# The order of the experts: from the fifth slot on, many and few tokens by turns in place of falling counts

## The chip, the cores and the metric

The kernel runs on one core of one Trainium2 chip. The metric is the device time of one execution in microseconds (us). TensorE is called PE here, VectorE DVE, ScalarE ACT, GpSimd POOL and SyncE SP.

## The reference: one layer of a hybrid decoder, with experts at its end

The layer takes 1024 prompt tokens and 8 tokens of decoding, 1032 rows of 1024 numbers. It norms them, projects them, runs gated linear attention and differential attention, projects back and adds. Then comes the part that the change touches, a mixture of experts: each token chooses one of 4 groups and in it 2 of 4 experts, so that 2064 pairs of token and expert are computed.

```
g = argmax(t @ w_rg + b_rg)
top_v, top_i = top_k(t @ w_re[g] + b_re[g], 2)
gates = softmax(top_v) * p_top
hid = silu(t @ w_gate[e]) * (t @ w_up[e])      # 1024 -> 256, for each chosen expert e
out = sum over e of gates[e] * (hid @ w_down[e])   # 256 -> 1024
x = x + out;  y = rmsnorm(x)
```

Only the tokens of an expert have to be computed for it. The counts of the 16 experts follow from the inputs; they are 140, 69 and 114 for the experts 0 to 2, and of the other thirteen, in falling order, 207, 170, 161, 152, 145, 135, 118, 116, 112, 112, 106, 105 and 102.

## The kernel before

Everything up to the router (about 700 us) is left alone by the change. After it the kernel runs 16 slots, one expert each, written out for every engine with semaphores between them. The experts 0 to 2 have the slots 0 to 2. The other thirteen are ranked on the chip by their number of tokens, and slot 3 takes the one with most, slot 15 the one with fewest. The columns of three tables on the chip go by rank: `tok` (which rows of the tokens to gather), `dest` (where to add the result) and `gtab` (the gate's weight); `sexp` holds the expert's number of each rank.

What is fixed when the kernel is built is the capacity of each slot, `CAPS` (line 38): 208 for the slots 0 to 2, then 212, 200, 188, 176, 164, 152, 140 and from slot 10 on 128. A capacity over 128 means two parts (`parts`, line 116), the second holding the rest: two gathers, two scatters, two parts of the down product. Tokens beyond a capacity would go to an overflow pass, which isn't taken with these inputs as the ranks' counts are all within it.

A slot e does the following, each engine in this order:

- SP (L747) loads the weights in f32, 3 MB per expert in three transfers, into two staging buffers: gate and up for slot e+3 once those of slot e+1 are split, down for slot e+2 once that of slot e is split.
- POOL issues the gather for slot e+3 (L918, from `h_scratch` in HBM, rows of 4 KB), then the scatter of slot e (L930, which adds rows of 4 KB into `sum_scratch` in HBM). A scatter waits for the slot's outputs and for the landing of the scatter before it, since two may add to the same row. So the gather for slot e+3 stands behind the scatter of slot e-1.
- PE computes gate and up for slot e (`split_mm`, L2101 to L2103: three f16 matmuls for one f32 product; 96 matmuls with as many columns as the capacity), transposes the tokens of slot e+1 (L2464, L2467), and computes the down product of slot e-1 (12 matmuls of 512 columns for each part). The second half of the transposes lies within the down product.
- ACT makes silu's exponentials (L1301 to L1305), the high half of the hidden product (L1309), reads half of the transposed tokens (L1291), splits weights for slot e+2 (L1233) and down for slot e+1 (L1238) into f16, and writes half of the output (L1323).
- DVE makes the hidden product (L1977, L1979), its low half (L1982), reads the other half of the tokens (L1965), writes half of the output (L1992) and makes the low halves of the split weights (L1803, L1808; three of 2.3 us per slot).

Two of PE's waits depend on the capacity. A slot of 128 needs one PSUM bank for gate and up (`one_bank`, line 131), and two such slots in a row use different banks, so that the second may start before the hidden product of the first is made (`hidden_before`, line 557). Otherwise gate and up of slot e wait for the hidden product of slot e-1.

After slot 15's scatter has landed, `sum_scratch` is loaded again, normed and written out.

Of the kernel before, what the change touches and what calls it, by code (L numbers as in the profile page):

```python
# [15 lines left out]
ALU = mybir.AluOpType  # L16
# [3 lines left out]
P = 128  # L20
D = 1024
# [12 lines left out]
NG, EPG, NE = 4, 4, 16  # L34
FF = 256
FIXED = 3
CAP_TOP, CAP_STEP = 212, 12
CAPS = [208] * FIXED + [max(P, CAP_TOP - CAP_STEP * j) for j in range(NE - FIXED)]
CAP = max(CAPS)
MORE = 80  # L40
FULL = FIXED + 1
# [108 lines left out]
def build(nc, I, O):  # L150
    ctx = ExitStack()
    with ctx:
# [131 lines left out]
        tok = sb("tok", [P, COLS + NOV], I32)  # L284
# [351 lines left out]
        def _(sp):  # L636
# [103 lines left out]
            def expert(e):  # L740
                if e < FIXED:
                    return slice(e, e + 1)
                return bass.ds(sp.value_load(sexp[0:1, e:e + 1], min_val=0, max_val=NE - 1), 1)

            def load(w, sub, x, s, sems):
                src = I[w][0, x].rearrange("e (k p) f -> p (e k) f", p=P)
# [72 lines left out]
        def _(pool):  # L819
# [93 lines left out]
            def gather(e):  # L913
                if e >= 2:
                    pool.wait_ge(s_eT, 4 * (e - 1))
                for g, r in parts(e):
                    rows_at = bass.IndirectOffsetOnAxis(ap=tok[0:r, 2 * e + g:2 * e + g + 1], axis=0)
                    pool.indirect_dma_start(out=xg[0:r, e % 2, g, :], out_offset=None, in_=h2d[:, :],  # L918
                                            in_offset=rows_at, bounds_check=T, oob_is_err=False
                                            ).then_inc(s_gx[e % 2], 16)  # L920

            def scatter(e):
                pool.wait_ge(s_ya, e + 1)
                pool.wait_ge(s_yv, e + 1)
                if e:
                    pool.wait_ge(s_yo[(e - 1) % 2], y_sent(e - 1))
                else:
                    pool.wait_ge(s_x1o, 16 * (NT + 1))
                for g, r in parts(e):
                    pool.indirect_dma_start(out=sumd[:, :], out_offset=bass.IndirectOffsetOnAxis(  # L930
                        ap=dest[0:r, 2 * e + g:2 * e + g + 1], axis=0), in_=yb[0:r, e % 2, D * g:D * g + D],
                        in_offset=None, bounds_check=T - 1, oob_is_err=False, compute_op=ALU.add
                        ).then_inc(s_yo[e % 2], 16)

# [36 lines left out]
        def _(act):  # L971
# [322 lines left out]
            def slot(e):  # L1294

                s = e % 2
                if e != NE:
                    c = CAPS[e]
                    g = eg[:, 0:2 * c]
                    act.wait_ge(s_gup, e + 1)  # L1300
                    act.activation(g, gate_up(e)[0], ACT.Exp, scale=-ISC2).then_inc(s_sg, 1)  # L1301
                    act.wait_ge(s_sg, 3 * e + 1)
                    act.activation(g, g, ACT.Ln, bias=1.0).then_inc(s_sg, 1)
                    act.wait_ge(s_sg, 3 * e + 2)
                    act.activation(g, g, ACT.Exp, scale=-1.0).then_inc(s_sg, 1)  # L1305
                    if e != NE - 1:
                        read_tokens(e + 1, 0)
                    act.wait_ge(s_hf, e + 1)
                    act.activation(hidh[:, s, :, 0:c], hid[:, 0:2 * c].rearrange("p (f t) -> p f t", f=2),  # L1309
                                   ACT.Copy).then_inc(s_hh2, 1)  # L1310
                    if e != NE - 1:
                        read_tokens(e + 1, 2)
                if e + 2 < NE:
                    split_gate_up(e + 2, 0)
                if e != 0:
                    v = e - 1
                    if e == 1:
                        act.wait_ge(s_route, 1)
                    if e >= 3:
                        act.wait_ge(s_yo[v % 2], y_sent(e - 3))  # L1320
                    for g, r in parts(v):
                        act.wait_ge(s_down, downs(e - 2) + 2 * g + 1)
                        ins = act.activation(yb[0:r, v % 2, D * g:D * g + 512], ps[0:r, 4 + 2 * g, :], ACT.Copy,  # L1323
                                             scale=gtab[0:r, 2 * v + g:2 * v + g + 1])
                    ins.then_inc(s_ya, 1)
                if e + 2 < NE:
                    split_gate_up(e + 2, 1)
                if e + 1 < NE:
                    if e != 0:
                        act.wait_ge(s_down, downs(e - 1))  # L1330
                    split_down(1 - s, 16 * ((e + 1) // 2 + 1))
# [50 lines left out]
        def _(dve):  # L1382
# [585 lines left out]
            def slot(e):  # L1968
# [17 lines left out]
                if e != 0:  # L1986
                    v = e - 1
                    if e >= 3:
                        dve.wait_ge(s_yo[v % 2], y_sent(e - 3))
                    for g, r in parts(v):  # L1990
                        dve.wait_ge(s_down, downs(e - 2) + 2 * g + 2)
                        ins = dve.tensor_scalar(yb[0:r, v % 2, D * g + 512:D * g + D], ps[0:r, 5 + 2 * g, :],  # L1992
                                                gtab[0:r, 2 * v + g:2 * v + g + 1], None, ALU.mult)
                    ins.then_inc(s_yv, 1)
                if e == 0:
                    dve.wait_ge(s_mlo, 4)
# [586 lines left out]
```

## Time and profile before

| | us |
|---|---|
| median of 3 runs | 966.47 |
| the runs | 966.39 to 970.37 |
| the profiled execution | 968.47 |
| its span, first to last instruction | 966.6 |
| slot 4's gate and up done | 775.91 |
| slot 15's gate and up done | 920.03 |
| last scatter issued | 931.45 |

All times in the text are from the start of the span. In the rows PE's busy time is modelled for pipelined matmuls: the start of one to the start of the next is the better measure. A timeline row has the start, the duration, engine and line, the operation with its operands, and in brackets the idle time of the engine before it with what released it.

### The profile page before, as it was taken

The numbers are of one execution on the slowest core, as the hardware profiler recorded it, in microseconds if no ns is written. First come the engines' busy times: TensorE is split into PE (matmuls) and PEld (weight loads), VectorE is DVE, ScalarE is ACT, GpSimd is POOL, SyncE is SP. The second block draws the span as 40 slices with busy tenths as digits, with TensorE's granted clock in tenths as the row PEclk, the third lists the DMA queues.
The fourth block names the chain that finished last, engine by engine and source line by source line (L and its number), as shares of the span: only waits on it lengthen the run. The fifth ranks groups of instructions, "written<-read, shape, count | busy, mean of one in ns | idle before, by whom it ended". The sixth has DMA issues, their size and how long they took to land.

```text
span 966.6 us, 16039 instructions
## 1 busy us (share of the span) xinstructions
PE 829.1 (86%) x6150; PEld 522.9 (54%) x6150; DVE 573.4 (59%) x932; ACT 424.8 (44%) x767; POOL 262.6 (27%) x173
## 2 busy tenths in 40 slices
PE   4999989779989989977899999995289999997920
PEld 3766634346556644324566755552277878765710
DVE  6632687747774531158788734335675767776815
ACT  5520230245651311235567614433436666775714
POOL 2104993640521000002000000000424465443312
PEclk9999999979998999996899999998579999998975
DMA  8326766301031268863000024423866889999647
GB/s 298 90 65 198 238 222 201 126 0 45 1 93 50 83 223 247 254 236 110 1 1 2 1 76 164 135 108 114 287 210 208 270 265 298 314 295 335 187 96 307
DMA packets 99073, 155.86 MB, mean 161 GB/s; under 512 B 13704, under 2 KB 63384, under 8 KB 98994
## 3 DMA queue, kind: packets, MB, share of 16 engines
q1 hardware_dynamic: 91170, 132.92, 41.6%
q0 software_dynamic: 6208, 18.17, 7.7%
q10 hardware_dynamic: 1616, 3.70, 1.0%
q8 instruction: 50, 0.82, 0.4%
q14 instruction: 29, 0.24, 0.1%
HBM read 129.25 MB, written 28.86 MB: 164 GB/s over the span
## 4 chain that ended last, share of the span: by engine, by line
PE 47%; DVE 12%; DMA 12%; issue 10%; SPq 7%; ACT 6%; POOL 6%; POOLq 0%; ACTq 0%; DVEq 0%
PE ps L2101 12%; PE ps L2102 11%; PE ps L2103 11%; DMA sum_scratch<-kv,dest 5%; POOL kv L860 4%; SPq L727 3%; SPq L728 2%; PE ps L2383 2%; DMA hT_reg<-h_scratch,tok 2%; DVE w_reg L1418 2%; DMA w_reg<-in_w_up 2%; DVE mxs L1725 2%; DMA gt<-q_scratch 1%; DVE dg_reg L2093 1%; PE ps L2371 1%
## 5 line engine op out<-in xcount | busy, mean ns | idle before, releaser
L930 POOL DMA_INDIRECT sum_scratch<-kv,dest x26 | 72.2, 2777 | 117.4 <-DMA sum_scratch<-kv,dest 74.5
L2101 PE MATMUL ps<-hT_reg,w_reg 128*128 128x344 f16 (+1 forms) x312 | 98.1, 314 | 4.6 <-DVE hT_reg L1430 2.7
L2102 PE MATMUL ps<-hT_reg,w_reg 128*128 128x344 f16 (+1 forms) x312 | 98.0, 314 | 0.0
L2103 PE MATMUL ps<-hT_reg,w_reg 128*128 128x344 f16 (+1 forms) x312 | 97.8, 313 | 0.0
L860 POOL TENSOR_TENSOR kv<-kv,gt 128x1024 f32<-128x1024 f32 x32 | 82.9, 2621 | 53.4 <-DMA kv<-in_cache_k 53.4
L2101 PE MATMUL ps<-w_reg,hT_reg 128*128 128x512 f16 (+1 forms) x216 | 83.5, 386 | 8.6 <-ACT kv L1099 4.9
L2102 PE MATMUL ps<-w_reg,hT_reg 128*128 128x512 f16 (+1 forms) x216 | 83.4, 386 | 0.0
L2103 PE MATMUL ps<-w_reg,hT_reg 128*128 128x512 f16 (+1 forms) x216 | 83.0, 384 | 0.0
L888 POOL TENSOR_TENSOR rst<-rst,neghalf 128x1 f32<-128x1 f32 (+3 forms) x27 | 18.8, 698 | 233.3 <-DVE rst L1706 233.3
L1195 ACT ACTIVATE hT_reg<-ps,mxn 128x128 f32<-128x128 f32 (+7 forms) x64 | 47.1, 739 | 50.0 <-DVE mxn L1726 46.3
L2101 PE MATMUL ps<-hT_reg,dg_reg 128*128 128x128 f16 (+4 forms) x256 | 55.1, 239 | 1.4 <-DVE hT_reg L1965 1.4
L1471 DVE TENSOR_REDUCE gbc<-kv 128x16 f32<-128x1024 f32 x32 | 38.6, 1215 | 29.5 <-POOL kv L860 29.5
L2101 PE MATMUL ps<-hT_reg,mix_reg 128*128 128x128 f16 (+5 forms) x256 | 54.3, 238 | 2.1 <-DVE hT_reg L1965 2.1
L2102 PE MATMUL ps<-hT_reg,dg_reg 128*128 128x128 f16 (+4 forms) x256 | 55.1, 239 | 0.0
L2103 PE MATMUL ps<-w_reg,mix_reg 128*128 128x512 f16 (+1 forms) x144 | 54.6, 379 | 0.0
L2101 PE MATMUL ps<-w_reg,mix_reg 128*128 128x512 f16 (+1 forms) x144 | 54.6, 379 | 0.0
L2102 PE MATMUL ps<-w_reg,mix_reg 128*128 128x512 f16 (+1 forms) x144 | 54.6, 379 | 0.0
L2103 PE MATMUL ps<-hT_reg,mix_reg 128*128 128x128 f16 (+5 forms) x256 | 54.2, 238 | 0.0
L2102 PE MATMUL ps<-hT_reg,mix_reg 128*128 128x128 f16 (+5 forms) x256 | 54.2, 238 | 0.0
L1725 DVE TENSOR_REDUCE mxs<-ps 128x1 f32<-128x640 f32 (+7 forms) x48 | 45.7, 951 | 10.2 <-PE ps L2349 7.0
L1445 DVE TENSOR_SCALAR dg_reg<-ps 128x512 f32<-128x512 f32 (+2 forms) x16 | 9.9, 619 | 64.6 <-PE ps L2103 64.6
L2383 PE MATMUL ps<-dg_reg,hT_reg 128*128 128x128 f32 x288 | 41.4, 293 | 4.3 <-DVE mix_reg L620 2.7
(379 smaller groups left out, 2117.1 us busy)
## 6 DMA issues: line engine op xcount, KB each, us to landing
kv<-in_cache_k SPq DMA_DIRECT2D x64, 256.0 KB, 3.2
w_reg<-in_w_gate SPq DMA_DIRECT2D x16, 1024.0 KB, 5.7
w_reg<-in_w_up SPq DMA_DIRECT2D x16, 1024.0 KB, 13.3
w_reg<-in_w_down SPq DMA_DIRECT2D x16, 1024.0 KB, 14.0
w_reg<-in_w_in SPq DMA_DIRECT2D x12, 1024.0 KB, 7.4
mix_reg<-in_cache_v SPq DMA_DIRECT2D x32, 256.0 KB, 3.2
kv<-in_cache_v SPq DMA_DIRECT2D x32, 256.0 KB, 3.2
mix_reg<-in_x_prompt SPq DMA_DIRECT2D x8, 512.0 KB, 8.5
```

The source lines that it names most:

```text
L727: page = sp.value_load(ptab[0:1, i:i + 1], min_val=0, max_val=n_pool - 1)
L728: sp.dma_start(vq[VBUF[k]][:, j], cv[bass.ds(page, 1)].rearrange("n p c -> p (n c)")).then_inc(s_vp[VBUF[k]], 16)
L860: pool.tensor_tensor(pg, pg, qbc[:, b % 2].unsqueeze(1).to_broadcast([P, 2, 512]), ALU.mult).then_inc(s_kq, 1)
L930: pool.indirect_dma_start(out=sumd[:, :], out_offset=bass.IndirectOffsetOnAxis(ap=dest[0:r, 2 * e + g:2 * e + g + 1], axis=0), in_=yb[0:r, ...
L1195: act.activation(prob[:, u % 3, m, 0:n], scores(u, m), ACT.Exp, scale=DK ** -0.5 * ISC2, bias=mxn[:, u % 2, m:m + 1], accum_out=rsum[:, i ...
L1418: dve.scalar_tensor_tensor(w_slot(slot_l, n), w_stage(n), SC, w_slot(slot_h, n), ALU.mult, ALU.subtract).then_inc(s_wl, 1)
L1471: dve.tensor_reduce(dsc[:, b, 2 * s:2 * s + 2], kv4[:, s].rearrange("p (g m d) -> p g m d", g=2, m=8), AX, ALU.add).then_inc(s_kh, 1)
L1725: link(dve.tensor_reduce(mxs[:, u % 2, ms], sc, AX, ALU.max))
L2101: pe.matmul(out, lh, rh, start=start, stop=False)
L2102: pe.matmul(out, lh, rl, start=False, stop=False)
L2103: return pe.matmul(out, ll, rh, start=False, stop=stop)
L2383: ins = pe.matmul(ps[:, 6 + i % 2, DV * h:DV * h + DV], wT[:, v % 2, j], vd[:, j, DV * h:DV * h + DV], start=j == 0, stop=j == i)
```

## The change

The ranks and their capacities stay, now as `RANKED`. A new list `PLACE` says which rank each slot takes: 0, 1, 2, 3, 4, 10, 5, 11, 6, 12, 7, 13, 8, 14, 9, 15. `CAPS` of the slots follows from it: 208, 208, 208, 212, 200, 128, 188, 128, 176, 128, 164, 128, 152, 128, 140, 128. Where a table is read, its column is now that of the slot's rank. The gathers, the scatters, the loads and the matmuls are otherwise the same ones.

```
-CAPS = [208] * FIXED + [max(P, CAP_TOP - CAP_STEP * j) for j in range(NE - FIXED)]
+RANKED = [208] * FIXED + [max(P, CAP_TOP - CAP_STEP * j) for j in range(NE - FIXED)]
+PLACE = [0, 1, 2, 3] + [r for pair in zip(range(4, 10), range(10, NE)) for r in pair]
+CAPS = [RANKED[r] for r in PLACE]
...
-                return bass.ds(sp.value_load(sexp[0:1, e:e + 1], min_val=0, max_val=NE - 1), 1)
+                return bass.ds(sp.value_load(sexp[0:1, PLACE[e]:PLACE[e] + 1], min_val=0, max_val=NE - 1), 1)
...
-                    rows_at = bass.IndirectOffsetOnAxis(ap=tok[0:r, 2 * e + g:2 * e + g + 1], axis=0)
+                    rows_at = bass.IndirectOffsetOnAxis(ap=tok[0:r, 2 * PLACE[e] + g:2 * PLACE[e] + g + 1], axis=0)
...
-                        ap=dest[0:r, 2 * e + g:2 * e + g + 1], axis=0), in_=yb[0:r, e % 2, D * g:D * g + D],
+                        ap=dest[0:r, 2 * PLACE[e] + g:2 * PLACE[e] + g + 1], axis=0), in_=yb[0:r, e % 2, D * g:D * g + D],
...
-                                             scale=gtab[0:r, 2 * v + g:2 * v + g + 1])
+                                             scale=gtab[0:r, 2 * PLACE[v] + g:2 * PLACE[v] + g + 1])
...
-                                                gtab[0:r, 2 * v + g:2 * v + g + 1], None, ALU.mult)
+                                                gtab[0:r, 2 * PLACE[v] + g:2 * PLACE[v] + g + 1], None, ALU.mult)
```

## Rows read from the trace of the kernel before

**Rows 1.** The page's slices, 40 equal ones: the DMA engines' busy tenths.
```profile
DMA  8326766301031268863000024423866889999647
```
**Rows 2.** Windows: stretch, its us, busy of each engine, clock, DMA share, GB/s.
```profile
775.91:790.99 15.08, 14.64 (x157) 11.82 (x154) 10.84 (x10) 10.02 (x11) 9.53 (x5) 1.00 0.87 277
...
859.96:872.10 12.14, 11.89 (x136) 8.32 (x136) 9.84 (x11) 9.13 (x11) 6.01 (x3) 1.00 0.96 283
...
883.08:898.95 15.87, 11.93 (x128) 8.95 (x129) 9.78 (x11) 8.80 (x11) 7.10 (x4) 0.78 1.04 345
...
909.31:920.03 10.72, 9.34 (x125) 7.19 (x123) 7.27 (x9) 4.98 (x9) 1.56 (x1) 1.00 0.46 68
...
776.00:909.00 133.00, 122.69 (x1401) 92.96 (x1398) 98.16 (x96) 92.95 (x107) 63.46 (x33) 0.97 0.97 302
```
**Rows 3.** Timeline of PE, slots 10 to 12.
```profile
863.84 0.38 PE L2101 MATMUL ps<-mix_reg,gt 128*12 128x512 f16 x1
...
866.53 0.23 PE L2101 MATMUL ps<-hT_reg,mix_reg 128*128 128x128 f16 x1
...
871.85 0.22 PE L2103 MATMUL ps<-hT_reg,mix_reg 128*128 128x128 f16 x1
874.03 0.62 PE L2464 MATMUL ps<-ident,hT_reg 128*128 128x128 f16 x8 [1.96 <-DMA hT_reg<-h_scratch,tok]
...
877.52 0.22 PE L2101 MATMUL ps<-hT_reg,dg_reg 128*128 128x128 f16 x1
```
**Rows 4.** Timeline of PE behind slot 12's gate and up.
```profile
887.02 1.03 PE L2464 MATMUL ps<-ident,hT_reg 128*128 128x128 f16 x8 [3.98 <-DMA hT_reg<-h_scratch,tok]
...
892.95 0.38 PE L2102 MATMUL ps<-mix_reg,gt 128*128 128x512 f16 x1
```
**Rows 5.** What PE waited for, 775 to 930: us in total, times, longest.
```profile
PE ps L2464 <- DMA hT_reg<-h_scratch,tok: 8.4, 5, 4.0
```
**Rows 6.** Timeline of POOL: scatters (L930) and one gather (L918).
```profile
785.56 6.52 POOL L930 DMA_INDIRECT sum_scratch<-kv,dest  x1 [4.63 <-DMA sum_scratch<-kv,dest]
...
802.86 4.22 POOL L930 DMA_INDIRECT sum_scratch<-kv,dest  x1 [6.29 <-DMA sum_scratch<-kv,dest]
807.38 1.51 POOL L930 DMA_INDIRECT sum_scratch<-kv,dest  x1 [0.30 <-issue]
...
873.20 2.25 POOL L930 DMA_INDIRECT sum_scratch<-kv,dest  x1 [6.62 <-DMA sum_scratch<-kv,dest]
875.75 1.37 POOL L930 DMA_INDIRECT sum_scratch<-kv,dest  x1 [0.30 <-issue]
877.43 1.09 POOL L918 DMA_INDIRECT hT_reg<-h_scratch,tok  x1 [0.31 <-issue]
884.35 2.66 POOL L930 DMA_INDIRECT sum_scratch<-kv,dest  x1 [5.84 <-DMA sum_scratch<-kv,dest]
...
895.27 2.80 POOL L930 DMA_INDIRECT sum_scratch<-kv,dest  x1 [6.89 <-DMA sum_scratch<-kv,dest]
...
915.69 1.56 POOL L930 DMA_INDIRECT sum_scratch<-kv,dest  x1 [7.03 <-DVE kv L1992]
924.67 1.56 POOL L930 DMA_INDIRECT sum_scratch<-kv,dest  x1 [7.42 <-DVE kv L1992]
931.45 1.56 POOL L930 DMA_INDIRECT sum_scratch<-kv,dest  x1 [5.21 <-DMA sum_scratch<-kv,dest]
```
**Rows 7.** Timelines of DVE and, between its two rows, of ACT.
```profile
788.30 2.28 DVE L1808 SCALAR_TENSOR_TENSOR mix_reg<-w_reg,mix_reg 128x2048 f16<-128x2048 f32 x1
...
833.48 0.42 ACT L1301 ACTIVATE junk<-ps 128x304 f32<-128x304 f32 x1 [3.42 <-PE ps L2103]
...
835.42 0.47 DVE L1979 SCALAR_TENSOR_TENSOR junk<-ps,junk 128x304 f32<-128x304 f32 x1
```
**Rows 8.** DMA queues, 776 to 883: MB and share of 16 engines.
```profile
q1 hardware_dynamic: 17870, 23.47, 64.8%
q0 software_dynamic: 3030, 8.77, 32.5%
```

## The prediction

> **What bounds the kernel now.** I read the page's slices first. Up to 700 us nothing that the change touches runs; from 776 us to about 900 us the DMA engines are full [rows 1]. Then I cut the stage of the experts at the ends of the gate and up products, one stretch for each slot (a stretch ends where ScalarE's first activation of that slot, L1301, starts). Slot 4's products are done at 775.91, slot 15's at 920.03. Look at the busy time of PE beside the sum: 14.64 of 15.08 us in slot 5, but 11.93 of 15.87 in slot 13, and beside it the DMA share, 0.97 from 776 to 909 [rows 2]. So PE sets the pace of the slots with two parts, and something with the DMAs that of the short ones at the end.
>
> What PE waits for there is named by the waits: the gather of the tokens, 8.4 us in five waits, 4.0 the longest [rows 5]. POOL's timeline tells why a gather is late [rows 6]. POOL issues, in order, the gather for slot e+3, then the scatter of slot e, and each scatter waits until the one before it has landed. The scatter of slot 9 was issued at 873.20 and 875.75, the gather behind it at 877.43, and PE could transpose at 887.02, after 3.98 us of idleness [rows 4, 6]. That is a third bound beside PE and the DMA engines: the chain of scatters, on whose back the gathers ride.
>
> **The work of the change, by engine.** The same 16 experts are computed with the same 16 capacities, so the counts of instructions stay: 26 gathers, 26 scatters, 48 loads, 96 matmuls per slot for gate and up. The look-up of the expert's number reads another column; the cost is nothing. Slots 0 to 4 keep their capacities. From slot 5 on the order 188, 176, 164, 152, 140, then six of 128, becomes 128, 188, 128, 176, 128, 164, 128, 152, 128, 140, 128.
>
> *PE alone.* Gate and up take 96 matmuls: 5.36 us at 128 columns (866.53 to the last at 871.85), so 0.042 us per column, 7.9 at 188 [rows 3]. Each part of the down product takes 2.6 to 2.7 us (863.84 to 866.53) [rows 3]. A short slot's transposes and down product take 3.49 us (874.03 to 877.52) [rows 3]. The stretch of slot e holds its own transposes (0.9 us, 1.5 with a second part), the down product of slot e-2 and its own gate and up; with 0.6 us of small waits this gives 15.0 for slot 5 of before (15.08 seen) and 12.0 for slot 11 (12.14 seen) [rows 2]. A short slot behind a short one needs 9.45. In the new order slot 5 needs 12.0, slots 6, 8, 10, 12 and 14 need 15.0, 14.5, 14.0, 13.55 and 13.05, and slots 7, 9, 11, 13 and 15 need 9.45 each: 129.4 us, to be set against 144.1 seen (132.0 by the same prices, the 2.6 between them being a down part that moves behind slot 15). The idle time on offer is therefore about 12 us, half of it in slot 13 alone.
>
> *The tail.* Slot 14 now has two parts. Behind slot 15's gate and up the next scatter came 4.64 us later (920.03 to 924.67) and the last 6.78 after it [rows 2, 6]. Add a down part (2.6) and a second scatter's issue (1.5 and a gap of 0.3): 15.8 instead of 11.4, 4.4 us more. The reload and final norm behind the last scatter stay as they are.
>
> *The DMA engines.* From 776 to 883 queue 1 moved 23.47 MB in 64.8% of 107 us, 2.95 us per MB; queue 0 moved 8.77 MB in 32.5%, 3.97 us per MB [rows 8]. A slot's weights (3.15 MB) need 9.3 us. Counting the tokens of each expert from the inputs, slots 3 to 15 of before have 207, 170, 161, 152, 145, 135, 118, 116, 112, 112, 106, 105 and 102; a row of 4 KB is gathered and scattered, so 112 rows need 3.6 us and 161 rows 5.2. A short slot asks for 12.9 us, a long one for 14.5. A pair asks for 27.4 where PE asks for 24.5. With 0.97 of 133 us used, the new order can fill 4 us at most.
>
> *The chain of scatters.* Slot 4's starts at 802.86, slot 9's at 873.20: five steps of two parts, 14.07 each. Slot 10's at 884.35, slot 11's at 895.27: a step of one part is 10.92 [rows 6]. A pair takes 25.0, more than PE's 24.5 to 22.5. Slots 0 to 4 are unchanged, so slot 4's scatter stays at 802.86; slot 14's then comes after five steps of either kind, 927.8. The weights are in by then, and the quiet steps were near 9 us (915.69 to 924.67), so I take 1.9 off: 925.9. The last follows after 6.78 + 1.8, at 934.5, against 931.45: 3.0 us later.
>
> *The gathers behind it.* The gather for slot 8 follows slot 4's scatter: both parts are issued by about 810.6, as long behind it as now (4.5 + 0.3 + 1.5, then the gathers), and land some 8 to 10 us later (877.43 to 887.02 is 9.6 [rows 4, 6]), say at 819. PE, faster by then, ends slot 7 at 775.91 + 12.0 + 15.0 + 9.45 = 812.4. It waits 6 us. The last such gather, slot 14's: slot 10's scatter at 802.86 + 3 x 14.07 + 3 x 10.92 = 877.8, gathers to 885.5, landed 895.1, then transposes 1.5, down 5.2 and gate and up 5.8: slot 14 done at 907.6, slot 15 at 917.1, and with the tail of 15.8 the end of the scatters is at 932.9.
>
> *The clock.* After PE had idled 3.98 us the granted clock of that stretch was 0.78, of levels 1.2 and 2.4 GHz, and the down product and transposes ran at half speed from 887.02 to about 893: 2.9 us lost [rows 2, 4]. After the 1.96 us at 874.03 it stayed whole [rows 3]. Waits of 6 us will cost that at least once in the last pairs: 932.9 becomes 935.8, 4.4 us later than now.
>
> *Bank sharing.* Two short slots in a row now use a bank each, and gate and up of a slot may start before the hidden product of the one before. No two are adjacent any more, so PE waits for it each time. Behind the products of a long slot PE has 3.5 us of transposes and one down part [rows 3], and the hidden product is there 2.4 us after the end of gate and up (slot 8, 833.48 to 835.42 + 0.47) [rows 7]. The 1.1 us between them hide it, so I cost it at nothing; were VectorE late by all of the 2.4, it would be 1.3 us for each of five slots, 6.5 in all, and it can't be a gain, since the matmuls may never start sooner for it.
>
> **Two rules of the Trainium skill.** Scatters of long slots take POOL several us: slot 3's from 785.56 for 6.52, ending 1.5 us after the third of the weight splits on VectorE (788.30 + 2.28) [rows 6, 7]. In the new order the scatters of the long slots again fall into these splits, so I keep 14.07 for the step; were POOL free of it as in the quiet tail (4.22 us against 1.56 [rows 6]), 2.7 us would go off each of five steps, the chain would end some 13 us earlier, and the DMA engines would be the limit. The Trainium skill ("SBUF — State Buffer", section "A bandwidth-pool intuition that's wrong (but worth ruling out)") says that GpSimd can't write its descriptors while VectorE holds the shared port. By that rule, too, the wait stays, and the trace agrees in kind; its wait behind VectorE's end is 0.1 us there, 1.5 here. The second rule is named with the first rival.
>
> **The rivals.** *The regimes mix and PE sets the pace.* For it: PE's 12 us of idleness lie nearly all in slots 10 to 15, where short slots stand together. Slot 15 would be done at 905.3 and the last scatter start at 921.1, 10.3 us sooner: 956.2. Against it: a DMA share of 0.97 and the order of POOL. Chance 0.17. The Trainium skill ("Perfetto Trace Analysis", section "Optimization Strategy") says that where the most-contended engine changes over time, interleaving the regimes may help; by that rule this rival is the outcome.
>
> *The clock falls in every pair (slower still).* Late gathers for slots 8, 10, 12 and 14 each leave PE idle for over 4 us, and each costs 2.9 us. The chain leaves PE 1.0, 1.5, 2.0 and 2.5 us per pair, so it loses 1.9, 1.4, 0.9 and 0.4, together 4.6 beyond the forecast: 975.1, up to 978 if scatters then start later as well. It decides as soon as the waits pass those 4 us in more than two pairs. Chance 0.25.
>
> *It washes out.* The chain's steps are shorter by 0.3 us each where less is transferred, the full 4 us of DMA time are filled, and the tail takes them back: 966.5, give or take 2. Chance 0.20.
>
> **The numbers.** The profiled execution took 968.47 us (span 966.6), the median of the runs is 966.47; the differences are the same on either. The two ways of counting give +3.0 and +4.4; I take +4.0, 970.5, nearer to the one with the clock in it; chance 0.38, own range 967.5 to 974. What a measurement can tell from no change is about 0.5%, so 961.6 to 971.3 is "same". Faster: the first rival, 0.17. Same: the wash and six tenths of the forecast, 0.43. Slower: the rest of the forecast and the second rival, 0.40. For 8 in 10 the range runs from 959 (into the first rival) to 978 (the second with its late scatters).
>
> **What would show it.** Right: PE idle before the transposes for slots 8, 10 or 12, released by the gather, 4 to 6 us each; scatter starts alternately 14 and 11 us apart from 802.9; DMA share about 1; two or more stretches with a granted clock under 0.85; 15 to 16 us from slot 15's products to the last scatter. Wrong: slot 7 ending at 812 with slot 8's tokens already there, steps of two parts near 11 us, or PE waiting for the hidden product. The steps carry the forecast: if those of two parts shrink to 12, it falls to the first rival.

## The result: slower, by a loop that the prediction did not close

| | before | changed |
|---|---|---|
| median of the runs, us | 966.43 | 980.04 |
| the runs, us | 965.17 to 970.37 | 974.36 to 983.11 |
| the profiled execution, us | 968.47 | 983.11 |
| its span, us | 966.6 | 981.3 |
| slot 4's products done | 775.91 | 776.29 |
| slot 15's products done | 920.03 | 932.68 |
| last scatter issued | 931.45 | 946.72 |

The ratio of changed to before is 1.0106, with a 95% interval from 1.0061 to 1.0151; the quotient of the two medians would be 1.0141, and the four runs of the changed kernel spread over 9 us. A repetition (below) gave 1.0193, from 1.0150 to 1.0236. So the changed kernel is slower by 1 to 2%. 970.5 was predicted, in a range that ended at 978: by the first ratio the result is 976.7, just inside it; by the median of 980.0 and by the repetition it lies past its end.

Between two executions of this kernel the work ahead of the experts may end some us apart, so the measure for a mechanism here is the *stage*: from the end of slot 4's products to the last scatter. It took 155.5 us before and 170.4 after, 14.9 more; the two spans differ by 14.7, so in the profiled executions all of the loss lies in it.

**The stage, slot by slot.** Windows of the changed kernel, cut where ScalarE's first activation of a slot starts. The columns are those of [rows 2]; the lines are slots 7, 9, 10, 11, 12 and 14, then the stretch of the last window of [rows 2], drawn out to 924.

```profile
803.20:816.62 13.42, 10.69 (x124) 8.16 (x124) 7.64 (x9) 9.20 (x10) 6.20 (x5) 0.87 1.06 330
...
831.31:841.25 9.94, 9.12 (x124) 7.08 (x121) 7.46 (x8) 8.90 (x11) 5.12 (x4) 1.00 1.04 285
841.25:862.06 20.81, 16.28 (x156) 12.19 (x157) 12.25 (x12) 9.73 (x12) 8.35 (x3) 0.84 0.84 280
862.06:871.84 9.78, 9.12 (x124) 7.08 (x121) 7.79 (x9) 8.82 (x10) 5.36 (x4) 1.00 1.01 282
871.84:892.53 20.69, 15.60 (x156) 11.45 (x157) 11.74 (x12) 9.65 (x11) 7.53 (x3) 0.84 0.79 272
...
902.16:922.72 20.56, 15.15 (x156) 10.95 (x157) 11.24 (x12) 9.56 (x11) 7.07 (x3) 0.83 0.56 176
...
776.00:924.00 148.00, 127.47 (x1408) 96.67 (x1407) 100.38 (x96) 94.47 (x110) 69.33 (x32) 0.92 0.87 272
```

Slots 9 and 11 took 9.94 and 9.78 us; the price of PE's work alone was 9.45. Slots 10, 12 and 14 took 20.81, 20.69 and 20.56 where that price was 14.0, 13.55 and 13.05, and slot 7 took 13.42 for 9.45. These four are 25.4 us over their prices, out of 27.0 for the eleven slots (156.4 seen, 129.4 priced). Before, the excess was 12.1 over 132.0 [rows 2]. So 2.6 us of work left the slots for the tail, and 14.9 us of idleness and half clock came in. Note the DMA share in the bad stretches, 0.84 and 0.79 (and 0.56 in slot 14, where the weights run out): in the stretches that lose the time, the engines that were to be full are not.

**Who PE waits for.** The waits of PE from 775 to 960 us (total, times, longest), and the four places on its timeline:

```profile
PE ps L2466 <- DMA hT_reg<-h_scratch,tok: 17.9, 4, 5.4
```
```profile
805.90 0.62 PE L2466 MATMUL ps<-ident,hT_reg 128*128 128x128 f16 x8 [2.74 <-DMA hT_reg<-h_scratch,tok]
...
845.78 0.29 PE L2466 MATMUL ps<-ident,hT_reg 128*128 128x128 f16 x1 [4.57 <-DMA hT_reg<-h_scratch,tok]
...
876.93 0.29 PE L2466 MATMUL ps<-ident,hT_reg 128*128 128x128 f16 x1 [5.12 <-DMA hT_reg<-h_scratch,tok]
...
878.29 0.63 PE L2103 MATMUL ps<-mix_reg,gt 128*128 128x512 f16 x1
...
881.92 0.38 PE L2103 MATMUL ps<-mix_reg,gt 128*128 128x512 f16 x1
...
907.57 0.29 PE L2466 MATMUL ps<-ident,hT_reg 128*128 128x128 f16 x1 [5.44 <-DMA hT_reg<-h_scratch,tok]
```

The counterpart of [rows 5]: 17.9 us in four waits, where it was 8.4 in five. The rest of the 25.4, 7.5 us, goes for the most part with the clock: after the wait of 5.12 us a matmul of 512 columns takes 0.63 us at 878.29 and 0.38 at 881.92, and the three long stretches show a granted clock of 0.83 and 0.84, a mean of stretches at the two levels of 1.2 and 2.4 GHz. What a whole clock gives back is measured below.

**Why the gather is late.** POOL's timeline, the counterpart of [rows 6], and DVE's behind it:

```profile
856.74 7.22 POOL L932 DMA_INDIRECT sum_scratch<-kv,dest  x1 [10.21 <-DVE kv L1994]
864.27 1.41 POOL L932 DMA_INDIRECT sum_scratch<-kv,dest  x1 [0.30 <-issue]
865.98 1.08 POOL L920 DMA_INDIRECT hT_reg<-h_scratch,tok  x1 [0.30 <-issue]
867.37 0.97 POOL L920 DMA_INDIRECT hT_reg<-h_scratch,tok  x1 [0.31 <-issue]
874.72 1.63 POOL L932 DMA_INDIRECT sum_scratch<-kv,dest  x1 [6.39 <-DMA sum_scratch<-kv,dest]
...
887.70 7.23 POOL L932 DMA_INDIRECT sum_scratch<-kv,dest  x1 [9.98 <-DVE kv L1994]
...
918.36 7.23 POOL L932 DMA_INDIRECT sum_scratch<-kv,dest  x1 [9.19 <-DVE kv L1994]
...
946.72 1.58 POOL L932 DMA_INDIRECT sum_scratch<-kv,dest  x1 [4.12 <-DMA sum_scratch<-kv,dest]
```
```profile
855.15 0.74 DVE L1994 TENSOR_SCALAR kv<-ps,gtab 48x512 f32<-48x512 f32 x1 [1.88 <-PE ps L2105]
855.82 4.47 DVE L1805 SCALAR_TENSOR_TENSOR mix_reg<-w_reg,mix_reg 128x2048 f16<-128x2048 f32 x2
860.22 2.28 DVE L1810 SCALAR_TENSOR_TENSOR mix_reg<-w_reg,mix_reg 128x2048 f16<-128x2048 f32 x1
...
886.11 0.74 DVE L1994 TENSOR_SCALAR kv<-ps,gtab 36x512 f32<-36x512 f32 x1 [1.87 <-PE ps L2105]
```

Read them as one circle. Slot 8's output is ready when DVE has written it (855.15 + 0.74); its scatter starts at 856.74. By then DVE has gone into three weight splits without a gap, and the scatter takes 7.22 us, until 1.46 us behind the end of the third (862.50). Before, a scatter of a long slot was released by a landing and met the splits midway, with 4.22 us left for it [rows 6]; here it is released by the output itself, each time at the splits' start. The gathers for slot 12 stand behind it, 865.98; PE gets the tokens at 876.93; with transposes and the down product of slot 10 its output is ready, and its scatter starts at 887.70. The circle is 9.24 + 10.95 + 10.77 = 30.96 us, the next one (887.70 to 918.36) 30.66. It leads from slot e to slot e+2, and PE's own work for two slots is 23.45 at that place (14.0 + 9.45). In the new order all long slots of the pairs are of one parity, so every turn of this circle has the two-part scatter, the two-part gather and two down parts in it, and the short slots between have no say.

### The profile page after: what moved, and what is told of

It is laid out like the page before. It is cut to its first block, busy times and chain, and to the rows that moved or that the text cites. A ratio compares the mean times of both kernels' runs of the same rounds, so it can differ in the third digit from the quotient of the medians.

```text
span 981.3 us, 16039 instructions
## 1 busy us (share of the span) xinstructions
PE 834.0 (85%) x6150; PEld 524.6 (53%) x6150; DVE 573.7 (58%) x932; ACT 426.1 (43%) x767; POOL 273.9 (28%) x173
## 4 chain that ended last, share of the span: by engine, by line
PE 45%; DMA 13%; issue 12%; DVE 11%; SPq 7%; POOL 6%; ACT 5%; POOLq 0%; ACTq 0%; DVEq 0%
PE ps L2103 11%; PE ps L2105 11%; PE ps L2104 11%; DMA sum_scratch<-kv,dest 6%; POOL kv L862 4%; DMA hT_reg<-h_scratch,tok 3%; SPq L729 3%; SPq L730 2%; PE ps L2385 2%; DVE w_reg L1420 2%; DMA w_reg<-in_w_up 2%; DVE mxs L1727 2%; DMA gt<-q_scratch 1%; DVE dg_reg L2095 1%; PE ps L2373 1%
## 5 line engine op out<-in xcount | busy, mean ns | idle before, releaser
L932 POOL DMA_INDIRECT sum_scratch<-kv,dest x26 | 82.8, 3186 | 118.9 <-DMA sum_scratch<-kv,dest 62.5
L2103 PE MATMUL ps<-hT_reg,w_reg 128*128 128x344 f16 (+1 forms) x312 | 99.3, 318 | 4.6 <-DVE hT_reg L1432 2.7
L2104 PE MATMUL ps<-hT_reg,w_reg 128*128 128x344 f16 (+1 forms) x312 | 99.2, 318 | 0.0
L2105 PE MATMUL ps<-hT_reg,w_reg 128*128 128x344 f16 (+1 forms) x312 | 99.1, 318 | 0.0
L2103 PE MATMUL ps<-hT_reg,dg_reg 128*128 128x208 f16 (+6 forms) x256 | 59.6, 245 | 0.8 <-DVE hT_reg L1967 0.8
L2104 PE MATMUL ps<-hT_reg,dg_reg 128*128 128x208 f16 (+6 forms) x256 | 59.5, 245 | 0.0
L2466 PE MATMUL ps<-ident,hT_reg 128*128 128x128 f16 x256 | 30.0, 240 | 27.0 <-DMA hT_reg<-h_scratch,tok 20.7
L2103 PE MATMUL ps<-hT_reg,mix_reg 128*128 128x128 f16 (+2 forms) x256 | 49.3, 230 | 2.5 <-DVE hT_reg L1967 2.4
L2104 PE MATMUL ps<-hT_reg,mix_reg 128*128 128x128 f16 (+2 forms) x256 | 49.3, 230 | 0.0
L2105 PE MATMUL ps<-hT_reg,mix_reg 128*128 128x128 f16 (+2 forms) x256 | 49.2, 229 | 0.0
```

The costliest lines, as they stand in the source:

```text
L2103: pe.matmul(out, lh, rh, start=start, stop=False)
L2104: pe.matmul(out, lh, rl, start=False, stop=False)
L2105: return pe.matmul(out, ll, rh, start=False, stop=stop)
L2466: ins = pe.transpose(bank16(kh)[:, c * k:c * k + P], xg[:, s, 0, col:col + P], ident16[:])
```

## The experiments

The theory is **the loop**: a scatter held by the splits on DVE, a gather queued behind it, PE waiting for that gather and then running at half clock. Its rivals: **the DMA engines** (their load in the pairs makes the landings late, wherever the gathers are issued), **the clock alone** (the waits are no worse than before but each costs half speed), **bank sharing** (PE waits for hidden products since no two short slots are adjacent), and **the order itself** (the longer tail and the uneven chain of scatters). The diffs are against the changed kernel, or against the kernel before where the heading says so.

### The changed kernel once more

> The changed kernel again, on the chip and in the rounds of the next three, since its four runs lay 9 us apart. Both theories: 8 to 14 us over the kernel before.

984.17 us beside 966.93; ratio 1.0193 [1.0150, 1.0236]. The waits for gathers are 18.7 us in six, 5.3 the longest; the stage is 171.4 us. POOL again (starts 29.9 and 30.8 us apart):

```profile
861.57 7.22 POOL L932 DMA_INDIRECT sum_scratch<-kv,dest  x1 [10.06 <-DVE kv L1994]
...
891.49 7.23 POOL L932 DMA_INDIRECT sum_scratch<-kv,dest  x1 [9.52 <-DVE kv L1994]
...
922.32 7.23 POOL L932 DMA_INDIRECT sum_scratch<-kv,dest  x1 [9.52 <-DVE kv L1994]
```

So the circle is no accident of one execution.

### Gathers ahead of the scatters, in the changed order and in the one before

```
             gather(2)
+            gather(3)
             for e in range(NE):
-                if e + 3 < NE:
-                    gather(e + 3)
+                if e + 4 < NE:
+                    gather(e + 4)
```

The gather that stood behind scatter e now stands ahead of it: this opens the circle, and no instruction is changed.

> The changed kernel with one gather more ahead of the loop, so that POOL issues the gather for slot e+4, not e+3, before the scatter of slot e. The tokens no longer ride behind a scatter that stands behind the weight splits. Theory A (late gathers, and the clock that falls after each): PE's four waits for a gather (17.9 us) go, the clock stays whole, and with them 7 us in each of the pairs 10/11, 12/13 and 14/15 and 4 us in slot 7; the pace is then the scatters' (25 us a pair) or PE's: 20 to 25 us under the changed kernel at most, 10 at least, so 955 to 970. Rival B (the DMA engines are full, the gathers would land late wherever they are issued): less than 4 us gained. Rival C (the waits for the shared bank): nothing gained.

> The same edit in the kernel before, with its falling order. Theory A: the waits of 8.4 us and the 2.9 us of half clock go, of which some come back as other waits behind the DMA engines: 955 to 960. With the first run it tells what the order alone is worth once the gathers are early: by PE's own pace 0, less the 4.4 us of the tail, so this one is faster than the changed one by 0 to 5 us. Rival B: within 3 us of before.

The changed order: 967.03 us beside 966.93, ratio 0.9982 [0.9955, 1.0008]; the stage shrinks from 171.4 to 150.2 us. The order before: 965.03, ratio 0.9986 [0.9964, 1.0008], stage 151.3. The waits of PE for gathers are gone in both. In the changed order the gain is 12 to 20 us by the ratios (0.9982 against 1.0106 and 1.0193), as the loop had it (10 to 25) and not as the rival of the full DMA engines (under 4). In the order before, the forecast of 955 to 960 was a miss: within 3 us of before is what that rival had given, so this second run alone doesn't speak against it. The changed order's window:

```profile
786.00:925.00 139.00, 130.02 (x1517) 98.45 (x1516) 105.17 (x104) 97.11 (x114) 57.74 (x31) 1.00 0.92 281
```

Clock 1.00 instead of 0.92, DMA share 0.92 instead of 0.87: the DMA engines carry the same traffic in less time when the gathers come early, so their load by itself doesn't set the pace. (How long these gathers took to land, no row shows, since nobody waited for them.) What the two orders differ by without the circle is nothing that this measurement can tell. One thing doesn't add up: the stages are 4 to 5 us shorter than that of the kernel before (155.5), the medians at most 2 us lower. In the profiled executions the difference lies ahead of the stage: the changed order's slot 4 was done at 781.74, that of the kernel before at 775.91, with the same matmuls in front of it. The difference is already there when slot 0 is done (717.31 against 711.54), ahead of all that the change touches; why is open.

### The hold taken away by another instruction

```
-                dve.scalar_tensor_tensor(dst, src, SC, hi, ALU.mult, ALU.subtract).then_inc(s_mlo, 1)
+                dve.tensor_scalar(dst, src, SC, None, ALU.mult).then_inc(s_mlo, 1)
...
-                dve.scalar_tensor_tensor(dst, src, SC, hi, ALU.mult, ALU.subtract).then_inc(s_mld, 1)
+                dve.tensor_scalar(dst, src, SC, None, ALU.mult).then_inc(s_mld, 1)
```

This leaves out the subtraction of the high half.

> The changed kernel with the low half of the split weights made by a tensor_scalar with one input (weight times 64) in place of a scalar_tensor_tensor with two; it leaves out the subtraction of the high half, so the output isn't the reference's. Theory A1 (VectorE's two-input splits keep POOL from writing its descriptors): the first scatter of a long slot takes 1.4 to 1.7 us, not 7.2, the gathers come 5 us sooner, and the kernel is 8 to 15 us faster than the changed one. Rival A2 (POOL waits for something else, or the one-input form holds it as well): these instructions stay at 5 to 7 us and the time within 3 us, unless the new instruction is itself shorter than 2.2 us.

962.20 us, ratio 0.9940 [0.9916, 0.9964], stage 147.1, no wait for a gather. The scatter that took 7.22 us, and the splits:

```profile
852.02 1.21 DVE L1805 TENSOR_SCALAR mix_reg<-w_reg 128x2048 f16<-128x2048 f32 x1
854.26 1.23 DVE L1805 TENSOR_SCALAR mix_reg<-w_reg 128x2048 f16<-128x2048 f32 x1 [1.04 <-issue]
856.16 1.23 DVE L1810 TENSOR_SCALAR mix_reg<-w_reg 128x2048 f16<-128x2048 f32 x1 [0.67 <-ACT mix_reg L1240]
...
853.23 2.35 POOL L932 DMA_INDIRECT sum_scratch<-kv,dest  x1 [7.81 <-ACT kv L1325]
```

As the loop says, and more than the 8 to 15 us that were expected (16 to 24 under the changed kernel by the ratios). But the edit does three things: the instruction reads one operand in place of two, it takes 1.21 us in place of 2.28, and since it is shorter the splits no longer follow without a gap: those at 854.26 and 856.16 start after 1.04 and 0.67 us of idleness. So it doesn't tell a hold by the form of the instruction from one by its length or by the missing gap. The next edit keeps form and length and changes the gap alone.

### The hold taken away by gaps, in both orders

```
                 dve.scalar_tensor_tensor(dst, src, SC, hi, ALU.mult, ALU.subtract).then_inc(s_mlo, 1)
+                if e >= 2:
+                    dve.wait_ge(s_mlo, 2 * e + j + 1)
```

DVE does all of its work, of the same form and length; it only waits for the end of each gate or up split before it issues the next one.

> The changed kernel with a wait on its own semaphore behind each of VectorE's first two weight splits, so that the three no longer run without a gap. Theory A1 (the port passes to POOL only where VectorE leaves a gap): the first scatter of a long slot takes at most 3.8 us (a split of 2.3 and 1.5), not 7.2; the loop scatter, gather, down product, scatter of the long slots falls from 31 us to 27, and the kernel is 8 to 12 us faster than the changed one. If POOL had to wait for the third split for another reason, nothing moves.

> The same two waits in the kernel before. Theory A1: first scatters of at most 3.8 us, the chain of scatters less far behind, its late gathers at slots 12 and 13 a few us earlier: 2 to 6 us faster than before. If the gaps themselves cost (0.1 us, twice a slot, on VectorE's 10 us of 14): within 1 us.

The changed order: 963.58 us beside 968.36, ratio 0.9952 [0.9923, 0.9981], stage 152.8. The order before: 964.34, ratio 0.9945 [0.9910, 0.9979], stage 150.7. Splits and scatter in the changed order:

```profile
788.49 2.28 DVE L1805 SCALAR_TENSOR_TENSOR dg_reg<-w_reg,dg_reg 128x2048 f16<-128x2048 f32 x1
790.80 2.29 DVE L1805 SCALAR_TENSOR_TENSOR gs_reg<-w_reg,dg_reg 128x2048 f16<-128x2048 f32 x1
```
```profile
789.43 2.84 POOL L932 DMA_INDIRECT sum_scratch<-kv,dest  x1 [6.79 <-DVE kv L1996]
...
827.54 2.81 POOL L932 DMA_INDIRECT sum_scratch<-kv,dest  x1 [8.09 <-DVE kv L1996]
```

The first split ends at 790.77, the second starts 0.03 us later, and the scatter is done at 792.27, 1.50 behind the first split; without the gap it was done 1.46 behind the third. No scatter takes over 2.86 us in either order, and no wait for a gather is left. That is the hold, by itself: a gap of 0.03 us lets POOL in. It makes the changed order faster than the kernel before, though nothing of its order, its tail or its traffic is touched. The gain over the changed kernel, 15 to 23 us by the ratios, is more than the 8 to 12 expected, which had counted with a turn of 27 us: the turns of the long slots' scatters were 24.3 and 25.7 us (854.68 to 879.01, and on to 904.70). In the order before the 4 us are within the 2 to 6 expected.

### The clock's share

In slots 9, 11 and 13, behind gate and up, where PE goes idle next:

```
+                    if e in (9, 11, 13):
+                        for _ in range(76):
+                            pe.matmul(ps[:, 0, 0:P], ones16[:], ones16[:], start=True, stop=True)
```

> The changed kernel with 76 spare matmuls of 128 columns (4.2 us, into a bank that nobody reads) ahead of the transposes in slots 9, 11 and 13, where PE waited 4.6 to 5.4 us for a gather; they change no result. Theory A (wait plus clock): the waits shrink to about 1 us, the granted clock of slots 10, 12 and 14 is 1.00 instead of 0.84, and each is 2 us shorter: 5 to 7 us less than the changed kernel. If the clock follows something else, it stays at 0.84 and nothing is gained; if the loop alone sets the pace and the slow clock lies in its shadow, the clock is whole and the gain under 2 us.

980.93 us beside 968.36, ratio 1.0126 [1.0073, 1.0180], stage 168.1. The stretches of slots 10, 12 and 14, here and in the repetition of the changed kernel:

```profile
847.73:867.91 20.18, 18.16 (x232) 14.83 (x230) 12.15 (x12) 9.67 (x11) 8.00 (x3) 1.00 0.82 274
877.70:895.90 18.20, 17.68 (x232) 14.29 (x230) 11.65 (x12) 9.61 (x11) 7.53 (x3) 1.00 0.91 311
...
905.53:924.10 18.57, 17.20 (x232) 13.76 (x230) 11.15 (x12) 9.55 (x12) 7.07 (x3) 1.00 0.60 194
```

They sum to 56.95 us; the repetition had 20.65, 19.65 and 20.71, 61.01. So with a whole clock (1.00) the three stretches are 4.1 us shorter and still 16.4 over their prices of 14.0, 13.55 and 13.05. Of their excess of 20.4 us the clock is a fifth; the circle is the rest. The forecast of 5 to 7 us for the whole was too high: PE still waited 2.0, 0.5 and 1.4 us behind the spare matmuls, the stage is 2.3 to 3.3 us shorter than in the two profiles of the changed kernel, and the ratio (1.0126 against 1.0106 and 1.0193) can't tell a gain from none.

### Bank sharing taken from the kernel before

```
-    return 4 * CAPS[e] <= 512
+    return False
```

> The kernel before with no slot taken as of one bank, so that gate and up of every slot wait for the hidden product of the one before, as they do in the changed kernel. The prediction costs it at nothing: within 0.3% of before. Rival C: up to 6.5 us slower, 1.3 for each of five slots.

970.42 us beside 969.27, ratio 1.0009 [0.9976, 1.0043], stage 157.8. The six short slots in a row lose what the change takes from them, and it costs nothing that can be told (the interval ends at 4 us, and the loss to be explained is 10 to 19). This rival falls.

### Other places for the short slots

```
-PLACE = [0, 1, 2, 3] + [r for pair in zip(range(4, 10), range(10, NE)) for r in pair]
+PLACE = [0, 1, 2, 3, 4, 10, 11, 5, 6, 12, 13, 7, 8, 14, 9, 15]
```

Two short ones and two long ones by turns, so that a circle over two slots always has one of each.

> The changed kernel with PLACE 0 1 2 3 4 10 11 5 6 12 13 7 8 14 9 15: long and short slots are still mixed as evenly, but two long, two short, so that the long ones no longer share the even slots. Theory L (a loop from slot e to e+2: the scatter of e, the gather of e+4 behind it, the transposes, the down product of e+2 behind these, the scatter of e+2; 31 us for a long slot, about 21 for a short one, against 24 of PE for two slots): the loops average 26, so the late gathers shrink or go, and it lies within 5 us of before, 8 to 12 us under the changed kernel. Rival M (mixing costs in itself, by the chain of scatters at 25 us a pair): as slow as the changed kernel, give or take 3.

977.91 us beside 968.36, ratio 1.0089 [1.0057, 1.0120]. A clear miss: that the circle's mean over two slots settles the time would have brought it back to the kernel before. It lies where the rival had put it, that mixing costs in itself; what speaks against that rival is the changed order above, mixed as well, which loses nothing once the circle is opened. Two waits for gathers of 8.3 and 8.2 us are in its profile, and one row shows what I had left out:

```profile
802.31 1.08 POOL L920 DMA_INDIRECT hT_reg<-h_scratch,tok  x1 [0.30 <-issue]
803.69 7.76 POOL L920 DMA_INDIRECT hT_reg<-h_scratch,tok  x1 [0.31 <-issue]
811.75 1.64 POOL L932 DMA_INDIRECT sum_scratch<-kv,dest  x1 [0.30 <-issue]
```

Here the second half of a gather meets the splits (DVE's start at 803.88) and is held for 7.76 us. The hold falls on whatever POOL is issuing, and with two long slots in a row a gather takes it undiluted. (The profiled execution took 985.5 us, some 8 above the median, so its rows count here and not its length.) So the parity of the long slots is one way into the trouble, not the only one, and the part of my theory that blames the parity is weaker than the part on the hold.

### Half of the weights' traffic

```
+                kk = src.shape[1] // (2 if now[0] >= 5 else 1)
-                sp.dma_start(mst[s][:, 2048 * sub:2048 * (sub + 1)].rearrange("p (k f) -> p k f", k=src.shape[1]),
-                             src).then_inc(sems[s], 16)
+                sp.dma_start(mst[s][:, 2048 * sub:2048 * (sub + 1)].rearrange("p (k f) -> p k f", k=src.shape[1])[:, 0:kk],
+                             src[:, 0:kk]).then_inc(sems[s], 16)
```

From slot 5 on half of each weight tile is loaded; the other half keeps older values.

> The changed kernel with half of each weight transfer from slot 5 on; the other half of the staged weights is left from earlier slots, so the output isn't the reference's. It takes 4.7 of 13 to 14.5 us of DMA work from each slot. Theory L (the loop of the long slots sets the pace by latencies): the 7.2 us that POOL is held stay, only the gather's landing of 9 to 10 us shortens by 2 to 4, so the waits for gathers in the long slots' loop shrink from 5 us to 1 to 3, and the kernel is 5 to 12 us faster than the changed one, not faster than before by more. Rival B (the DMA engines' share sets the pace): no waits, 15 us or more under the changed kernel.

966.18 us beside 969.27, ratio 0.9989 [0.9954, 1.0025], stage 153.1. Its waits for gathers and its window:

```profile
PE ps L2471 <- DMA hT_reg<-h_scratch,tok: 6.8, 4, 2.1
```
```profile
776.00:900.00 124.00, 113.72 (x1308) 86.36 (x1306) 94.08 (x94) 90.61 (x105) 63.35 (x30) 0.99 0.72 204
```
```profile
851.28 4.33 POOL L937 DMA_INDIRECT sum_scratch<-kv,dest  x1 [7.88 <-DMA sum_scratch<-kv,dest]
...
875.97 4.98 POOL L937 DMA_INDIRECT sum_scratch<-kv,dest  x1 [7.17 <-DMA sum_scratch<-kv,dest]
...
900.46 7.23 POOL L937 DMA_INDIRECT sum_scratch<-kv,dest  x1 [6.93 <-DVE kv L1999]
```

The engines stand at 0.72, and PE still waits four times for its gathers, some 3 us less each time; with waits of 2 us the clock stayed at 0.99. The landing got shorter, as expected: the gather for slot 12 was issued at 857.62 and its tokens were there at 865.08, 7.5 us in place of 10.95. But the hold did not stay, as the expectation had it. From slot 5 on, only slot 12's scatter, released by its output, was held for 7.23 us; those of slots 6, 8 and 10 were released by a landing and took 5.79, 4.33 and 4.98. Less traffic shortens two parts of the circle, so this run doesn't tell them apart. Its gain over the changed kernel, 11 to 20 us by the ratios, is above the 5 to 12 given for the loop and reaches the 15 of the rival, whose sign, no waits, did not come. So the traffic does lengthen the circle. But with half of the weights gone the stage is no shorter than with the gaps (152.8) or with the early gathers (150.2), which leave the traffic whole. The engines' fullness by itself isn't the bound.

### Both repairs together

Gaps and early gathers, in the changed order and in the one before:

> The changed kernel with both edits, the gaps between VectorE's splits and the gathers one slot earlier. If what is left behind the gaps is the chain of scatters and the DMA engines, the earlier gathers add nothing: as with the gaps alone, 0.995 of before. If late gathers still cost: 0.990.

> The falling order with both edits. Same two cases, 0.995 or 0.990 of before. Against the run before it, it is the price of the order alone once POOL isn't held: by the tail 4 us for the changed order, by what the gaps alone gave (0.9952 and 0.9945) nothing.

The changed order: 961.59 us beside 969.27, ratio 0.9910 [0.9876, 0.9944], stage 147.7. The order before: 964.00, ratio 0.9945 [0.9912, 0.9977], stage 150.4. The first is the fastest of the kernels here that compute the whole layer. Its window:

```profile
781.00:920.00 139.00, 131.95 (x1531) 99.68 (x1532) 107.81 (x107) 98.37 (x117) 52.84 (x31) 1.00 0.93 286
```

PE is busy for 131.95 of 139 us. Its slots 5 to 15 take 133.9 us (779.01 to 912.94) where the price was 129.4; in the order before with the same two edits they take 138.8 (780.16 to 918.97), and the longer tail of the new order gives 2.2 us of that back. Which of the two expected cases it is, 0.990 or 0.995, the intervals leave open for the changed order; the order before has the same ratio as with the gaps alone. With POOL free the new order is at least as good as the old one; the two intervals overlap, so whether it is better by the 2.4 us between the medians isn't settled.

## Why the prediction was right and wrong, point by point

The direction was right (slower), and so were the kind of PE's waits and the place of the trouble, the scatters with the gathers behind them. The forecast of 4 us was too small: the medians differ by 13.6, the ratio gives 10.2. That the range reached as far as 976.7 is due to the second rival, whose sum came near for a reason that was only in part its own (see the clock).

**The step that failed: 14.07 us for a two-part step of the chain of scatters.** It was taken from scatters that were released by a landing and had 4.22 us of hold left [rows 6]. The prediction saw the hold (6.52 us at slot 3, ending 1.5 behind the third split [rows 6, 7]) and kept 14.07 all the same. When the scatter is released by its own output, the hold is 7.22, and the step from slot 8's to slot 9's is 17.98 (856.74 to 874.72). The step of one part behind it was too short as well: 12.98 (874.72 to 887.70) for 10.92, since it ended with PE's late output and not with a landing. From slot 4 on the steps were 12.44, 11.86, 16.31, 13.55, 17.98, 12.98, 18.46 and 12.20, where 14 and 11 by turns were forecast. A pair took 30.96 and 30.66 us, not 25.0: over the last pairs that is the loss.

**And the form of the sum.** The scatters were treated as a chain in which PE only has to have delivered. The rows show a circle: PE's wait makes its output late, and that output is what releases the next scatter. A shortfall of the chain against PE (0.5 to 2.5 us in a pair by the prediction's numbers) isn't lost once and hidden after; every turn that is longer than PE's two slots is a wait again. The runs with the early gathers and with the gaps open this circle at two different places, and each takes the whole loss away.

**Where the waits fall.** Forecast: 6 us before the transposes of slot 8, at 819, as PE ends slot 7 at 812.4. Seen: PE had waited 2.74 us for slot 7's tokens, ended slot 7 at 816.62, and those of slot 8 were there. The kind of wait was right, the first place was a slot off. Slots 10, 12 and 14 then had waits of 4.57, 5.12 and 5.44, within the 4 to 6 given.

**The clock.** "At least once" was too low: three stretches at 0.83 and 0.84 (the sign given for it, two or more under 0.85, came true). That is the condition of the second rival, waits over 4 us in more than two pairs, and its bounds of 975.1 to 978 lie nearest to the result. But the 4.6 us that it added to the forecast were made of clock alone, and that term was too high: 2.9 us each, where the rows give 2.0 to 2.2 (stretch less price less wait: 6.81 - 4.57, 7.14 - 5.12, 7.51 - 5.44) and the run that kept the clock up 1.4. What it left out is larger: the waits themselves, 17.9 us, which it took as covered by the chain's 25 us a pair. That its bounds lie nearest is in part luck.

**The DMA engines.** "Full, 4 us to be had": the share over the stage is 0.87, and 0.79 to 0.84 in slots 10 and 12, so they did not hold the changed kernel. With both repairs slots 5 to 15 took 133.9 us where the kernel before took 144.1, 10 us less and not 4. The 27.4 us that a pair was to ask of them was too high: slots 10 and 11 took 24.37 us together (841.26 to 865.63), with a share of 1.04 and PE busy for 23.24. There the engines are full and the pair is 0.9 us over PE's price of 23.45; whether they take that 0.9 no run shows.

**The tail.** Forecast 15.8 us, 4.4 more than before; seen 14.04 (932.68 to 946.72), 2.6 more. The direction was right.

**PE's prices and the banks.** Slots without a wait came within 0.5 us of their prices (9.94 and 9.78 for 9.45). Bank sharing at nothing was right, as far as the run that takes it from the order before can tell.

**The rule on the shared port.** A held scatter ends 1.46 us behind the third split, and with a gap behind the first one 1.50 behind that: POOL gets in where DVE pauses, and between instructions that follow without a gap it mostly didn't. The Trainium skill ("SBUF — State Buffer", section "A bandwidth-pool intuition that's wrong (but worth ruling out)") describes this, beside a `tensor_copy`, as a DMA waiting for descriptors that GpSimd can't write until VectorE releases the shared port. The trace agrees in kind, with a delay of 1.5 us in place of its 0.1. The prediction cited it and then left the price of the hold as it was. It also wrote down the sum with the hold away, a chain some 13 us shorter and the DMA engines as the limit, and dismissed it; the kernel with both edits went that way, though at a pace near PE's.

**The first rival.** That mixing the regimes helps where nothing else binds: 956.2 was its figure, 961.59 the best that was reached, after two other edits. Of the 12 us of PE's idleness that the order was to fill, the changed kernel filled nothing as it stood.

**Left open.** Why in slots 11 and 12 of the kernel before the scatter got in within 2.80 us [rows 6] although its splits follow as closely (and in slot 5 of the changed kernel within 3.10, ahead of the third split's end). Why the stages of the runs with early gathers are shorter by more than their medians are. Whether the new order is worth 2 us once both repairs are in.

## What to carry to other kernels

Before you mix long and short items, look for the circle that ties item e to item e+2 through the buffers and queues, add up one whole turn of it from rows, and set it against the engine's work for as many items; if some circle holds only the long items, the short ones between them fill nothing. A stall read off in one order belongs to the moment at which its instruction was released: ask what will release it in the new one. Where a queue issues transfers that someone waits for soon behind ones that no one waits for, turn them around first.

## What the runs showed of the hardware

An indirect DMA that POOL issues just as DVE starts three f32 splits of 2.28 us with two operands and no gap is held until 1.46 us after the last (7.22 to 7.26 us for a scatter, in the profiles of all eight kernels here whose splits have neither the gap nor the one operand, if only for slot 0 in four of them; two gathers were held for 7.76 and 7.90 us, until 0.9 us after the last). It isn't always so: a few scatters got in behind the first or second split (2.44 to 3.10 us) with splits as close, and the condition isn't known. A wait of DVE on its own semaphore, which leaves 0.03 us between two of them, lets POOL in after the first (2.84 us; the four kernels with gaps have one scatter of 3.64 us and none other over 2.88). That wait alone made the changed kernel 1.5 to 2.4% faster (0.9952 against 1.0106 and 1.0193) and the one before 0.5%. With one operand (1.21 us each, with pauses between many of them) the first scatter of a slot took 1.6 to 3.2 us.
